# Splitting operands ahead of a stage boundary, and multiplying the first output tile there

## The chip, the cores and the metric

The kernel runs on one core of a Trainium2 chip. The metric is the device time of one execution in microseconds. Besides, one execution was recorded by the hardware profiler; its times are those of the profile.

## The reference

One step of a hybrid decoder layer on a prompt of 1024 tokens and on 8 samples of 4 tokens, all in float32. A combined input projection feeds a gated DeltaNet group (4 heads) and a differential attention group (4 heads). What the change touches is the step after it, in which the outputs of the eight heads are joined and multiplied with `w_out`:

```python
h = x + jnp.concatenate([o_g, o_d], axis=-1) @ w_out          # (L, 1024) @ (1024, 1024)
hn = _rmsnorm(h, ffn_norm_g)
u, new_ffn = _causal_dwconv(hn @ w_up, ffn_buf, ffn_conv_w, ffn_conv_b)
y = h + (jax.nn.silu(u[..., :D_FF]) * u[..., D_FF:]) @ w_down
```

## The kernel before

The kernel holds everything with features on the 128 partitions and tokens along the free axis: `T` = 1056 columns, of which the last 32 are the samples. It has four phases that follow each other with a barrier of all engines: projection, DeltaNet and attention of the prompt, `sample_stage`, and `output_and_mlp`. A product in float32 is made of three products of rounded parts: an operand is split into `hi` (a cast on ScalarE) and `lo` (a subtraction on VectorE), and TensorE adds hi·hi, hi·lo and lo·hi. `SEQ` is 1024, `TG` 352, `KT` 8, `H` 4.

`sample_stage` (L1750) computes the samples' DeltaNet and paged attention, and beside it normalises and gates the head outputs of the prompt in three groups of columns (`norm` on VectorE, `gate` on GpSimd). Each engine's order is written out by hand. Near its end TensorE does `multiply(0)`, `turn_map(1)`, `turn_out(0)`, `multiply(1, ...)`, `turn_out(1)`, `sum_few(1)`. Each of these waits in the queue for ScalarE or VectorE: `turn_out(1)` for `keep_out(1)` on ScalarE, and `sum_few(1)` for `add_rows(1)` on VectorE and `square_few(1)` on ScalarE. After it, `root_few(1)` and `norm_few(1)` end the phase. SyncE loads the first two tiles of `w_out` (`w_raw`, 512 KB each) during it. Before the barrier the stage splits weight tile 0 (L2362, L2575) and head 0 over all columns (L2366, L2579).

`output_and_mlp` (L2585) begins with the output projection, in 16 units. Unit u makes output tile u % 8 for the token half u // 8 (528 columns, `HB`), with 48 matmuls of 264 columns (L3452): 8 heads, three products, two PSUM banks. Weight tiles have two buffers: SyncE loads tile u once `low(u-2)` is done, ScalarE casts it (`high(u)`, L2936), VectorE subtracts (`low(u)`, L3152), and TensorE's `unit(u)` waits for `split_lo`. Here the heads 1 to 7 are split over all 1056 columns first (`o_high`, L2939, and `o_low`, L3178), while unit 0 follows head by head; then comes the split of tile 1. After a unit VectorE adds the residual (`residual(u)`) and sums squares (`gather(u)`). SyncE's queue at the phase's start, which the change leaves as it is:

```python
for u in range(NO):
    if u >= 2:
        load(u)
    if u < 2:
        for t in ((0,), range(1, KT))[u]:
            sp.dma_start(hT[:, t, :], x_scratch[:, t, :]).then_inc(x_in[u], 16)
    if u in ROWS_AT:
        load_rows(ROWS_AT.index(u))
```

So eight loads of x_scratch of 528 KB and three small loads of rows stand ahead of `load(2)`. At units 2, 4, 6 and 7 TensorE also transposes rows (`turn_rows`). The MLP's up-projection follows, then the down-projection.

Of the kernel before, what the change touches and what calls it, by code (L numbers as in the profile page):

```python
# [22 lines left out]
P = 128  # L23
D = 1024
KT = D // P
# [88 lines left out]
def hybrid_step(nc, i, o):  # L114
# [64 lines left out]
    held.append(S_out)  # L179
    phase(sample_stage, i, o, c, feat, ba, key_in, z_scratch, S_out, o_hi, o_lo)  # L180
    c["free"] = c["w_out_end"]
    phase(output_and_mlp, i, o, c, feat, o_hi, o_lo, o_at, feat_at, w_out_at, h_scratch, g_scratch, x_scratch)


# [1564 lines left out]

def sample_stage(nc, i, o, c, feat, ba, key_in, z_scratch, S_out, o_hi, o_lo, sem):  # L1750

# [22 lines left out]
        m.sb(f"s_{n}", [P, NS]) for n in ("ET", "A", "AT", "PT", "I_AT", "I_AA", "fold", "far"))  # L1774
    DT = m.sb("s_DT", [P, P])
    q_rows = m.sb("s_q_rows", [P, H, NB * WP])
    assert m.top >= c["free"] + 4 * T
# [33 lines left out]
    mask_few = mapT[0:NS, 0, 0:NBT * NR].rearrange("p (t r) -> p t r", t=NBT)  # L1811
    mask = m.sb("p_mask", [P, NBT, NS])
    sign_row = m.sb("p_sign_row", [1, P])
    sign = m.sb("p_sign", [P, 1])
# [4 lines left out]
    sq = [late.sb(f"o_sq{x}", [P, TG]) for x in range(2)] + [e[x][:, 0:TG] for x in range(2)]  # L1819
    sq_few = [sq[t][:, 0:H * SB * NL].rearrange("p (h n) -> p h n", h=H) for t in range(NBT)]  # L1820
    o_junk = sq[0][:, 0:DH]
# [4 lines left out]
    z_few = late.sb("o_z_few", [P, H, NS])  # L1826
    roots = late.sb("o_roots", [P, TG])
    roots_hi = [late.sb(f"o_roots_hi{x}", [P, TG], F32R) for x in range(2)]
    roots_lo = [late.sb(f"o_roots_lo{x}", [P, TG], F32R) for x in range(2)]
    head_out = [feat[:, t if t < H else 2 * H + t, :] for t in range(NH)]  # L1830
    zT = feat[:, 4 * H:5 * H, 0:SEQ]
    GROUPS = [slice(0, TG), slice(TG, 2 * TG), slice(2 * TG, SEQ), slice(SEQ, T)]

    bank_a, bank_b = m.ps("s_bank_a", [P, 512]), m.ps("s_bank_b", [P, 512])
    key_ps = [m.ps(f"p_key_ps{x}", [P, 512]) for x in range(2)]
# [20 lines left out]
    w_in, w_high = [sem(f"o_w_in{n}") for n in range(2)], sem("o_w_high")  # L1856
    gated_few, head_high = sem("o_gated_few"), sem("o_head_high")
    z_in, z_few_in, z_made, strip_zero, strip_made, spread_made = (
# [52 lines left out]
    with nc.Block() as block:  # L1911
# [115 lines left out]
        def _(pe):  # L2027
# [79 lines left out]
            def turn_delta():  # L2107
                pe.wait_ge(dve_done, DV["o_scaled"])
                nc.tensor.transpose(bank_b[:, 0:P], o_rows[:, :], c["ident"][:, :]).then_inc(pe_done, 1)

# [90 lines left out]
            def spread_roots(use):  # L2201
# [50 lines left out]
            turn_out(0)  # L2252
            multiply(1, (turn_delta, lambda: sum_few(0)))
            turn_out(1)
            sum_few(1)

        @block.scalar
        def _(act):
# [54 lines left out]
            for b in range(NB):  # L2313
# [36 lines left out]
            def square_few(t):  # L2350
                act.wait_ge(out_added, H * (t + 1))
                nc.scalar.activation(sq_few[t], few(t), ACT.Square).then_inc(few_squared, 1)

# [18 lines left out]
        def _(dve):  # L2372
# [74 lines left out]
            def delta_gate():  # L2447
                dve.wait_ge(pe_done, PE["o_turned"])
                dve.wait_ge(z_made, H + 1)
                nc.vector.scalar_tensor_tensor(out=feat[:, 0:H, SEQ:T], in0=bank_b[:, 0:P].rearrange("p (h t) -> p h t", h=H),  # L2450
                                               scalar=c["gain"][:, 0:1], in1=z_few[:, :, :], op0=ALU.mult, op1=ALU.mult
                                               ).then_inc(gated_few, 1)
# [79 lines left out]
            for b in range(NB):  # L2532
# [32 lines left out]
                if b == 5:  # L2565
                    add_state(6)
                    add_state(7)
                    keep_map(0)
            maxes(1)
# [12 lines left out]
    m.free()  # L2582


def output_and_mlp(nc, i, o, c, feat, o_hi, o_lo, o_at, feat_at, w_at, h_scratch, g_scratch, x_scratch, sem):  # L2585

# [44 lines left out]

    pair = [m.ps(f"f_pair{b}", [P, 2, 512]) for b in range(4)]
    bank = [pair[b // 2][:, b % 2, :] for b in range(8)]
# [115 lines left out]
    with nc.Block() as block:  # L2749
# [178 lines left out]
        def _(act):  # L2928
            act.sem_inc(split_hi, CREDIT + 1)

# [7 lines left out]
            def o_high(t):  # L2938
                nc.scalar.copy(o_hi[:, t, :], head_out[t]).then_inc(o_hi_done, 1)  # L2939

# [13 lines left out]
            def x_high(name, j):  # L2954
                hi, lo = xop[name]
                if name in ("P1", "P2", "P3"):
                    n, x = (j if name == "P1" else HK + j), (1 if name == "P3" else 0)
                    act.wait_ge(scaled_h, KT * x + n + 1)
                    src = hT[:, n, halves[x]]
                    if name != "P3":  # L2960
                        act.wait_ge(o_lo_done, KT - 1)
                elif name == "P5":
                    act.wait_ge(t1_made, j + 1)
                    src = t1[:, j, :]
                elif name == "P4":
                    act.wait_ge(t4_made, j + 1)
                    src = hT[:, HK + j, one]
                else:
                    act.wait_ge(t2_made if name == "P6" else t3_made, j + 1)
                    src = hT[:, j, one if name == "P6" else two]  # L2970
                if name in ("P5", "P7", "P4", "P3"):
                    act.wait_ge(unit_done, NO)
                if name == "P6":
                    act.wait_ge(o_lo_done, KT - 1)
                nc.scalar.copy(hi[:, j, :], src).then_inc(x_hi_done[name], 1)

            def up_high(s):
# [5 lines left out]
                if s < WR:  # L2983
                    if s >= 3:
                        act.wait_ge(unit_done, NO)
                    else:
                        act.wait_ge(rows_turned, 4)
                else:
                    act.wait_ge(multiplied, s - WR + 1)
                nc.scalar.copy(wop[s % WR][0][:, :, :], W_OF[name]).then_inc(up_hi, 1)  # L2990

            for t in range(1, KT):
                o_high(t)
            high(1)
            nc.scalar.preload_act_table(ACT.Sqrt)
            for u in range(NO):
                square_of(u)
                if u + 2 < NO:
                    high(u + 2)
                if u == KT:  # L3000
                    roots(0)
# [143 lines left out]
        def _(dve):  # L3145
            sub, add, mult = ALU.subtract, ALU.add, ALU.mult
            dve.sem_inc(split_lo, CREDIT + 1)

# [27 lines left out]
            def o_low(t):  # L3176
                dve.wait_ge(o_hi_done, t)
                nc.vector.tensor_tensor(o_lo[:, t, :], head_out[t], r32(o_hi[:, t, :]), sub).then_inc(o_lo_done, 1)  # L3178

# [235 lines left out]
        def _(pe):  # L3415
# [25 lines left out]
            def unit(u):  # L3441
# [4 lines left out]
                for k in range(KT):  # L3446
                    if u == 0 and k:
                        pe.wait_ge(o_lo_done, k)
                    for x, (w, t) in enumerate(PARTS):
                        for b in range(2):  # L3450
                            a = half * HB + b * HQ
                            mm = nc.tensor.matmul(pair[s][:, b, 0:HQ], (w_hi, w_lo)[w][s][:, k, :], (o_hi, o_lo)[t][:, k, a:a + HQ],  # L3452
                                                  start=(k + x == 0), stop=(k == KT - 1 and x == 2))
# [169 lines left out]
```

## Time and profile before

| what | value |
|---|---|
| time, median of 3 runs | 1624.13 us (1623.47 to 1630.41) |
| the profiled execution | 1628.96 us |
| its span | 1627.4 us |
| TensorE matmuls busy | 1515.5 us, 93% |
| VectorE busy | 1054.6 us, 65% |
| ScalarE busy | 638.4 us, 39% |
| GpSimd busy | 395.5 us, 24% |
| mean granted TensorE clock | 0.968 |

The span runs from the first to the last recorded instruction; the rest of an execution lies around it. Times in the rows count from the start of the span. The granted clock is 1.00 at the full 2.4 GHz and 0.50 at 1.2 GHz.

### The profile page before, as it was taken

To read this page: it belongs to the slowest core of one execution; us is meant where nothing else is said; L and a number is where in the kernel's file an instruction comes from. 1 tells how busy PE (TensorE), PEld (TensorE's weight loads), DVE (VectorE), ACT (ScalarE), POOL (GpSimd) and SP (SyncE) were. 2 spreads that over 40 slices of the span, in tenths; PEclk is the share of its full clock that TensorE was granted. 3 is DMA by queue.
4 is the path that set the end of the run, shared out by engine and by line. 5 is a ranking of instruction groups with operands and counts; after the bars stand their busy time and mean duration, and the time that the engine had idled before them with its cause. 6 is when DMAs were issued, how large, how long until landed. Compare 5 with 4: busy or idle time off the path is not lost.

```text
span 1627.4 us, 30132 instructions
## 1 busy us (share of the span) xinstructions
PE 1515.5 (93%) x11911; PEld 1430.0 (88%) x11911; DVE 1054.6 (65%) x1575; ACT 638.4 (39%) x1102; POOL 395.5 (24%) x750
## 2 busy tenths in 40 slices
PE   7999999898688888788999799999999999999998
PEld 6999999898577777644898799999999999999998
DVE  7444389777557676456547988887878787534420
ACT  6434242332334443353423444444444445423222
POOL 4000166554432243153002322222222220000000
PEclk8999999999789999899899799999999999999999
DMA  6211111232112311185542122222222226745333
GB/s 220 97 48 52 28 47 35 87 100 92 31 37 54 105 25 38 46 328 156 193 148 93 53 78 79 71 78 72 77 80 79 82 92 207 262 159 198 132 107 108
DMA packets 177981, 165.63 MB, mean 102 GB/s; under 512 B 24245, under 2 KB 157163, under 8 KB 176184
## 3 DMA queue, kind: packets, MB, share of 16 engines
q1 hardware_dynamic: 173528, 154.30, 30.7%
q0 software_dynamic: 1664, 6.29, 1.0%
q10 hardware_dynamic: 2656, 3.21, 0.5%
q8 instruction: 90, 1.47, 0.4%
q14 instruction: 43, 0.35, 0.1%
HBM read 125.68 MB, written 37.96 MB: 101 GB/s over the span
## 4 chain that ended last, share of the span: by engine, by line
PE 47%; DVE 2%; issue 1%; DMA 1%; ACT 1%; SPq 0%; POOL 0%; ACTq 0%; DVEq 0%; POOLq 0%
PE f_pair L3498 27%; PE f_pair L3544 15%; PE f_pair L3452 3%; DMA w_raw<-in_w_out 1%; DVE feat L3194 0%; PE f_pair L3578 0%; ACT w_hi L2936 0%; DVE m_xP_lo L3208 0%; DMA up_raw<-in_w_up 0%; DVE feat L3213 0%; SPq L2800 0%; PE f_pair L3512 0%; PE f_pair L3421 0%; DVE feat L3160 0%; DVE w_lo L3152 0%
## 5 line engine op out<-in xcount | busy, mean ns | idle before, releaser
L3498 PE MATMUL f_pair<-m_xP_hi,up_w_hi 128*128 128x264 f32 x1232 | 254.6, 288 | 12.8 <-DVE m_xP_lo L3208 9.4
L3498 PE MATMUL f_pair<-m_xP_lo,up_w_hi 128*128 128x264 f32 x1232 | 252.5, 286 | 0.0
L3498 PE MATMUL f_pair<-m_xP_hi,up_w_lo 128*128 128x264 f32 x1232 | 252.3, 286 | 0.0
L195 PE MATMUL proj<-x_hi,win_hi 128*128 128x352 f32 x672 | 220.1, 327 | 0.0
L195 PE MATMUL proj<-x_hi,win_lo 128*128 128x352 f32 x672 | 217.3, 323 | 0.0
L195 PE MATMUL proj<-x_lo,win_hi 128*128 128x352 f32 x672 | 216.9, 323 | 0.0
L3498 PEld LDWEIGHTS f_pair<-m_xP_hi,up_w_hi 128*128 128x128 f32 x1232 | 192.9, 190 | 15.3 <-issue 10.2
L3498 PEld LDWEIGHTS f_pair<-m_xP_lo,up_w_hi 128*128 128x128 f32 x1232 | 193.0, 190 | 0.0
L3498 PEld LDWEIGHTS f_pair<-m_xP_hi,up_w_lo 128*128 128x128 f32 x1232 | 192.5, 190 | 0.0
L3544 PE MATMUL f_pair<-dn_g_hi,dn_w_hi 128*128 128x352 f32 x528 | 171.9, 325 | 0.2 <-DVE f_pre L3271 0.2
L3544 PE MATMUL f_pair<-dn_g_lo,dn_w_hi 128*128 128x352 f32 x528 | 169.7, 321 | 0.0
L3544 PE MATMUL f_pair<-dn_g_hi,dn_w_lo 128*128 128x352 f32 x528 | 169.4, 321 | 0.0
L195 PEld LDWEIGHTS proj<-x_lo,win_hi 128*128 128x128 f32 x672 | 127.7, 190 | 0.0
L195 PEld LDWEIGHTS proj<-x_hi,win_hi 128*128 128x128 f32 x672 | 127.3, 189 | 0.3
L195 PEld LDWEIGHTS proj<-x_hi,win_lo 128*128 128x128 f32 x672 | 127.3, 189 | 0.0
L769 DVE RECIPROCAL head_root<-head_root 128x352 f32<-128x352 f32 x48 | 112.5, 2345 | 15.5 <-ACT head_root L591 15.3
L3319 DVE SCALAR_TENSOR_TENSOR f_acc<-f_pre,f_col,f_acc 128x1072 f32<-128x1072 f32 x88 | 116.8, 1329 | 0.0
L3355 DVE TENSOR_TENSOR dn_w_lo<-dn_raw,dn_w_hi 128x1024 fp32r<-128x1024 f32 x50 | 61.2, 1224 | 69.9 <-ACT dn_g_hi L3097 69.5
L3544 PEld LDWEIGHTS f_pair<-dn_g_lo,dn_w_hi 128*128 128x128 f32 x528 | 100.0, 189 | 0.0
L3544 PEld LDWEIGHTS f_pair<-dn_g_hi,dn_w_hi 128*128 128x128 f32 x528 | 99.0, 187 | 0.5 <-DVE f_pre L3271 0.5
L3231 DVE TENSOR_TENSOR up_w_lo<-up_sums,up_w_hi 128x512 fp32r<-128x512 f32 x88 | 72.0, 820 | 42.2 <-ACT up_w_hi L2990 42.2
L3544 PEld LDWEIGHTS f_pair<-dn_g_hi,dn_w_lo 128*128 128x128 f32 x528 | 99.1, 188 | 0.0
(462 smaller groups left out, 2932.3 us busy)
## 6 DMA issues: line engine op xcount, KB each, us to landing
dn_raw<-in_w_down SPq DMA_DIRECT2D x50, 512.0 KB, 4.0
up_raw<-in_w_up SPq DMA_DIRECT2D x44, 512.0 KB, 4.6
win_raw<-in_w_in SPq DMA_DIRECT2D x28, 512.0 KB, 3.9
g_scratch<-f_prod SPq DMA_DIRECT2D x22, 528.0 KB, 2.7
dn_g_in<-g_scratch SPq DMA_DIRECT2D x66, 176.0 KB, 3.6
p_key<-in_cache_k SPq DMA_DIRECT2D x32, 256.0 KB, 3.7
w_raw<-in_w_out SPq DMA_DIRECT2D x16, 512.0 KB, 6.1
x_scratch<-feat SPq DMA_DIRECT2D x1, 4224.0 KB, 12.0
```

The lines of the kernel that those rows point to most:

```text
L195: mm = nc.tensor.matmul(out, w[:, k, :], x[:, k, g * TG:(g + 1) * TG], start=(k == 0 and i == 0), stop=(k == KT - 1 and i == 2))
L769: nc.vector.reciprocal(root[j % 2][:, :], root[j % 2][:, :]).then_inc(root_inverted, 1)
L3231: nc.vector.tensor_tensor(lo[:, :, :], W_OF[order(s // NP)[s % NP]], r32(hi[:, :, :]), sub).then_inc(up_lo, 1)
L3319: nc.vector.scalar_tensor_tensor(out=acc[s][:, 0:F_OUT], in0=pre[s][:, t:t + F_OUT], scalar=col[:, j, NB * F_PAD + t:NB * F_PAD + t + 1], ...
L3355: nc.vector.tensor_tensor(dw[s][1][:, 0, :], w_in[NTH_W[u] % NRAW][:, :], r32(dw[s][0][:, 0, :]), sub)
L3452: mm = nc.tensor.matmul(pair[s][:, b, 0:HQ], (w_hi, w_lo)[w][s][:, k, :], (o_hi, o_lo)[t][:, k, a:a + HQ], start=(k + x == 0), stop=(k == ...
L3498: mm = nc.tensor.matmul(pair[OF[name]][:, b, 0:HQ], w_[a][:, j, :], x_[t][:, j, b * HQ:(b + 1) * HQ], start=(name in FIRST_IN and j + x == ...
L3544: mm = nc.tensor.matmul(bank[f][:, 0:TG], w_[a][:, 0, f * P:(f + 1) * P], g_[t][:, 0, :], start=(k == KS[g][0] and x == 0), stop=(k == KS[ ...
```

## The change

The phase `sample_stage` now splits the first 528 columns of all eight heads (`split_one` on ScalarE and VectorE) and both loaded weight tiles, and TensorE does all of unit 0 in it (`first_unit`), in three pieces around `turn_out(1)` and `sum_few(1)`. Its PSUM tile `pair0` outlives the barrier. The sample stage's transposed DeltaNet output moves to another bank for this. `output_and_mlp` starts with the residual of unit 0 and with unit 1, and splits the second 528 columns of the heads one by one behind units 0 to 7 (`two_hi`, `two_lo`), since only unit 8 needs them. On ScalarE `high(2)` comes first there.

```diff
+    c["pair0"] = shared.ps("f_pair0", [P, 2, 512])
...
+            def first_unit(a, b):
+                if a == 0:
+                    pe.wait_ge(w_low, 1)
+                    pe.wait_ge(dve_done, DV["S7"])
+                for k in range(a, b):
+                    pe.wait_ge(one_low, k + 1)
+                    for x, (w, o_) in enumerate((("w_hi", one_hi), ("w_hi", one_lo), ("w_lo", one_hi))):
+                        for y in range(2):
+                            nc.tensor.matmul(c["pair0"][:, y, 0:HQ], c[w][0][:, k, :], o_[k][:, y * HQ:(y + 1) * HQ],
+                                             start=(k + x == 0), stop=(k == KT - 1 and x == 2))
...
             multiply(1, (turn_delta, lambda: sum_few(0)))
+            first_unit(0, 2)
             turn_out(1)
+            first_unit(2, 4)
             sum_few(1)
+            first_unit(4, KT)
...
+            def split_one(t):
+                act.wait_ge(gated, (2 if t < H else NG) * H)
+                act.wait_ge(normed, NH * 2)
+                if t >= H:
+                    act.wait_ge(fresh_scored, 2)
+                nc.scalar.copy(one_hi[t][:, :], head_out[t][:, 0:HB]).then_inc(one_high, 1)
+
+            for t in range(H):
+                split_one(t)
             exps(1)
+            for t in range(H, NH):
+                split_one(t)
             keep_out(0)
...
             root_few(0)
             act.wait_ge(gated_few, 1)
-            act.wait_ge(gated, H * NG)
-            nc.scalar.copy(o_hi[:, 0, :], head_out[0]).then_inc(head_high, 1)
+            act.wait_ge(normed, NH * NG)
+            act.wait_ge(w_in[1], 16)
+            nc.scalar.copy(c["w_hi"][1][:, :, :], c["w_raw"][1][:, :, :]).then_inc(w_high, 1)
             keep_out(1)
...
+            split_one(0)
+            split_one(1)
             maxes(1)
+            split_one(2)
             weigh(1)
+            split_one(3)
+            split_one(4)
             keep_map(1)
             add_rows(0)
             delta_norm()
-            dve.wait_ge(w_high, 1)
-            nc.vector.tensor_tensor(c["w_lo"][0][:, :, :], c["w_raw"][0][:, :, :], r32(c["w_hi"][0][:, :, :]), ALU.subtract)
+            split_one(5)
+            split_w(0)
             delta_gate()
             norm_few(0)
-            dve.wait_ge(head_high, 1)
-            nc.vector.tensor_tensor(o_lo[:, 0, :], head_out[0], r32(o_hi[:, 0, :]), ALU.subtract)
+            split_one(6)
+            split_one(7)
             add_rows(1)
+            split_w(1)
             norm_few(1)
...
         @block.scalar
         def _(act):
-            act.sem_inc(split_hi, CREDIT + 1)
+            act.sem_inc(split_hi, CREDIT + 2)
...
-            for t in range(1, KT):
-                o_high(t)
-            high(1)
+            high(2)
             nc.scalar.preload_act_table(ACT.Sqrt)
             for u in range(NO):
                 square_of(u)
-                if u + 2 < NO:
+                if 1 <= u < NO - 2:
                     high(u + 2)
+                if u < KT:
+                    o_high(u)
...
-            for t in range(1, KT):
-                o_low(t)
-            low(1)
             for u in range(NO):
                 residual(u)
                 gather(u)
                 if u + 2 < NO:
                     low(u + 2)
+                if u < KT:
+                    o_low(u)
...
                 for k in range(KT):
-                    if u == 0 and k:
-                        pe.wait_ge(o_lo_done, k)
+                    if u == KT:
+                        pe.wait_ge(o_lo_done, k + 1)
...
+            pe.sem_inc(unit_done, 1)
             for u in range(NO):
-                unit(u)
+                if u:
+                    unit(u)
```

## Rows read from the trace of the kernel before

**Rows 1.** The page, busy time of each engine.

```profile
PE 1515.5 (93%) x11911; PEld 1430.0 (88%) x11911; DVE 1054.6 (65%) x1575; ACT 638.4 (39%) x1102; POOL 395.5 (24%) x750
```

**Rows 2.** The chain that ended last: start, duration, what.

```profile
774.32 0.33 SPq L2800
...
779.53 10.37 DMA w_raw<-in_w_out
...
789.93 1.06 ACT w_hi L2936
791.01 1.24 DVE w_lo L3152
...
792.29 6.19 PE f_pair L3452 x48
...
905.36 5.97 PE f_pair L3498 x24
...
912.18 3.16 PE f_pair L3498 x24
```

**Rows 3.** Windows: stretch, its length, busy time by engine, granted clock, DMA share, GB/s.

```profile
774.40:784.90 10.50, 9.70 (x48) 9.02 (x48) 9.40 (x9) 9.14 (x9) 0.00 (x0) 0.63 0.92 357
784.90:792.20 7.30, 6.15 (x48) 5.93 (x48) 1.86 (x4) 1.69 (x2) 0.00 (x0) 1.00 0.90 241
792.20:884.80 92.60, 92.06 (x768) 91.12 (x768) 52.91 (x73) 29.67 (x44) 2.59 (x2) 1.00 0.42 131
...
774.40:782.20 7.80, 7.08 (x30) 6.77 (x31) 6.70 (x6) 7.80 (x8) 0.00 (x0) 0.50 0.88 335
905.40:911.90 6.50, 5.94 (x24) 5.33 (x24) 5.79 (x8) 6.47 (x12) 0.99 (x1) 0.50 0.00 0
...
342.00:345.20 3.20, 3.20 (x13) 3.20 (x12) 3.17 (x3) 0.33 (x1) 2.24 (x4) 0.50 0.55 150
771.90:774.40 2.50, 0.00 (x0) 0.00 (x0) 0.84 (x2) 0.32 (x2) 0.00 (x0) 0.51 0.00 0
```

**Rows 4.** DMA issues, 784 to 786 us: count, KB each, us from issue to landing.

```profile
w_raw<-in_w_out SPq DMA_DIRECT2D x1, 512.0 KB, 6.8
```

**Rows 5.** Timeline, end of the sample stage: start, duration, engine, line; in brackets idle time before.

```profile
768.60 0.60 PE L2174 MATMUL p_score<-p_key,p_mapT 128*32 128x512 f32 x2
768.70 1.26 DVE L2579 TENSOR_TENSOR o_lo<-feat,o_hi 128x1056 fp32r<-128x1056 f32 x1
769.26 0.59 ACT L2286 COPY p_e<-p_score 128x512 f32<-128x512 f32 x1 [0.59 <-PE p_score L2174]
...
769.90 0.66 PE L2184 MATMUL p_fresh_ps<-ident,p_e 128*128 128x128 f32 x4 [0.71 <-ACT p_e L2286]
770.60 0.48 DVE L2502 TENSOR_REDUCE feat<-p_fresh_ps 128x16 f32<-128x32 f32 x4 [0.64 <-PE p_fresh_ps L2184]
...
771.42 0.43 PE L2113 MATMUL p_key_ps<-o_sq,ones 128*128 128x64 f32 x2 [0.87 <-ACT o_sq L2352]
...
772.83 0.28 DVE L2458 SCALAR_TENSOR_TENSOR feat<-feat,gain,o_roots_few 128x64 f32<-128x64 f32 x1
...
774.41 0.81 PE L3452 MATMUL f_pair<-o_hi,w_hi 128*128 128x264 f32 x2 [2.55 <-DVEq L3147]
```

**Rows 6.** Instructions of two lines: count, shortest/median/longest ns, first and last start.

```profile
L2975 ACT CAST m_xP_hi<-feat x24: 626/628/632, 853.6 to 913.5; 128x528 fp32r<-128x528 f32 x24
...
L3208 DVE TENSOR_TENSOR m_xP_lo<-feat,m_xP_hi x24: 694/701/1814, 856.3 to 918.5; 128x528 fp32r<-128x528 f32 x24
```

**Rows 7.** Timeline of ScalarE and VectorE, 755 to 763 us, idle times where splits go.

```profile
758.67 0.69 ACT L2279 ACTIVATE p_e<-p_score,p_stat 128x512 f32<-128x512 f32 x1 [4.47 <-DVE p_stat L2474]
...
762.15 0.59 ACT L2286 COPY p_e<-p_score 128x512 f32<-128x512 f32 x1 [2.40 <-PE p_score L2174]
...
757.56 0.19 DVE L2469 TENSOR_TENSOR p_fresh<-p_fresh_ps,p_mask 128x32 f32<-128x32 f32 x1 [1.43 <-PE p_fresh_ps L2156]
...
762.81 0.88 DVE L2491 COPY p_mapT<-p_score 128x128 f32<-128x128 f32 x4 [1.94 <-PE p_fresh_ps L2164]
```

More of the change, by code:

```diff
@@ L179, in hybrid_step @@
     held.append(S_out)
-    phase(sample_stage, i, o, c, feat, ba, key_in, z_scratch, S_out, o_hi, o_lo)
+    shared = Memory(nc, keep.top)
+    c["pair0"] = shared.ps("f_pair0", [P, 2, 512])
+    phase(sample_stage, i, o, c, feat, feat_at, ba, key_in, z_scratch, S_out)
     c["free"] = c["w_out_end"]
-    phase(output_and_mlp, i, o, c, feat, o_hi, o_lo, o_at, feat_at, w_out_at, h_scratch, g_scratch, x_scratch)
+    phase(output_and_mlp, i, o, c, feat, o_at, feat_at, w_out_at, h_scratch, g_scratch, x_scratch)
 def ln_rows(ap):
@@ L1747, in delta_and_attention, with sample_stage @@
     m.free()
-def sample_stage(nc, i, o, c, feat, ba, key_in, z_scratch, S_out, o_hi, o_lo, sem):
+def sample_stage(nc, i, o, c, feat, feat_at, ba, key_in, z_scratch, S_out, sem):
     o_part = 4 * KT * T
@@ L1775, in sample_stage @@
     DT = m.sb("s_DT", [P, P])
+    q_rows_at = m.top
     q_rows = m.sb("s_q_rows", [P, H, NB * WP])
@@ L1796, in sample_stage @@
     NV = NB - 2
+    keyT_at = m_low.top
     keyT = [over_split.sb("p_keyT0", [P, H, PAST]), m_low.sb("p_keyT1", [P, H, PAST])]
@@ L1812, in sample_stage @@
     mask = m.sb("p_mask", [P, NBT, NS])
+    sign_at = m.top
     sign_row = m.sb("p_sign_row", [1, P])
@@ L1819, in sample_stage @@
     sq = [late.sb(f"o_sq{x}", [P, TG]) for x in range(2)] + [e[x][:, 0:TG] for x in range(2)]
-    sq_few = [sq[t][:, 0:H * SB * NL].rearrange("p (h n) -> p h n", h=H) for t in range(NBT)]
+    sq_few = [m.at(f"o_sq_few{t}", [P, H, SB * NL], F32, sign_at + 4 * H * SB * NL * t)[:, :, :] for t in range(NBT)]
     o_junk = sq[0][:, 0:DH]
@@ L1827, in sample_stage @@
     roots = late.sb("o_roots", [P, TG])
+    roots_at = late.top
     roots_hi = [late.sb(f"o_roots_hi{x}", [P, TG], F32R) for x in range(2)]
@@ L1830, in sample_stage @@
     head_out = [feat[:, t if t < H else 2 * H + t, :] for t in range(NH)]
+    HB = T // 2
+    HQ = HB // 2
+    ONE_LO = [q_rows_at + 4 * HB * x for x in range(2)] + [roots_at + 4 * HB * x for x in range(3)] + [keyT_at + 4 * HB * x for x in range(3)]
+    one_hi = [m.at(f"o_one_hi{t}", [P, HB], F32R, feat_at + 4 * T * (4 * H + t % H) + 4 * HB * (t // H)) for t in range(NH)]
+    one_lo = [m.at(f"o_one_lo{t}", [P, HB], F32R, at) for t, at in enumerate(ONE_LO)]
+    c["o_one"] = (one_hi, one_lo)
     zT = feat[:, 4 * H:5 * H, 0:SEQ]
     GROUPS = [slice(0, TG), slice(TG, 2 * TG), slice(2 * TG, SEQ), slice(SEQ, T)]
-    bank_a, bank_b = m.ps("s_bank_a", [P, 512]), m.ps("s_bank_b", [P, 512])
+    bank_a, bank_b = c["pair0"][:, 0, :], c["pair0"][:, 1, :]
     key_ps = [m.ps(f"p_key_ps{x}", [P, 512]) for x in range(2)]
@@ L1856, in sample_stage @@
     w_in, w_high = [sem(f"o_w_in{n}") for n in range(2)], sem("o_w_high")
-    gated_few, head_high = sem("o_gated_few"), sem("o_head_high")
+    gated_few, w_low = sem("o_gated_few"), sem("o_w_low")
+    one_high, one_low = sem("o_one_high"), sem("o_one_low")
     z_in, z_few_in, z_made, strip_zero, strip_made, spread_made = (
@@ L2108, in turn_delta @@
                 pe.wait_ge(dve_done, DV["o_scaled"])
-                nc.tensor.transpose(bank_b[:, 0:P], o_rows[:, :], c["ident"][:, :]).then_inc(pe_done, 1)
+                nc.tensor.transpose(key_ps[1][:, P:2 * P], o_rows[:, :], c["ident"][:, :]).then_inc(pe_done, 1)
             def sum_few(t):
@@ L2351, in square_few @@
                 act.wait_ge(out_added, H * (t + 1))
+                act.wait_ge(setup_ps, 1)
                 nc.scalar.activation(sq_few[t], few(t), ACT.Square).then_inc(few_squared, 1)
@@ L2449, in delta_gate @@
                 dve.wait_ge(z_made, H + 1)
-                nc.vector.scalar_tensor_tensor(out=feat[:, 0:H, SEQ:T], in0=bank_b[:, 0:P].rearrange("p (h t) -> p h t", h=H),
+                nc.vector.scalar_tensor_tensor(out=feat[:, 0:H, SEQ:T], in0=key_ps[1][:, P:2 * P].rearrange("p (h t) -> p h t", h=H),
                                                scalar=c["gain"][:, 0:1], in1=z_few[:, :, :], op0=ALU.mult, op1=ALU.mult
@@ L2568, in _, with split_one, split_w @@
                     keep_map(0)
+            def split_one(t):
+                dve.wait_ge(one_high, t + 1)
+                if t < 2:
+                    dve.wait_ge(pe_done, PE["qS"])
+                elif t < 5:
+                    dve.wait_ge(normed, NH * NG)
+                else:
+                    dve.wait_ge(scored, NB)
+                nc.vector.tensor_tensor(one_lo[t][:, :], head_out[t][:, 0:HB], r32(one_hi[t][:, :]), ALU.subtract).then_inc(one_low, 1)
+            def split_w(n):
+                dve.wait_ge(w_high, n + 1)
+                if n:
+                    dve.wait_ge(gated_few, 1)
+                    dve.wait_ge(normed, NH * NG)
+                nc.vector.tensor_tensor(c["w_lo"][n][:, :, :], c["w_raw"][n][:, :, :], r32(c["w_hi"][n][:, :, :]), ALU.subtract).then_inc(w_low, 1)
+            split_one(0)
+            split_one(1)
             maxes(1)
+            split_one(2)
             weigh(1)
+            split_one(3)
+            split_one(4)
             keep_map(1)
@@ L2573, in _, with output_and_mlp @@
             delta_norm()
-            dve.wait_ge(w_high, 1)
-            nc.vector.tensor_tensor(c["w_lo"][0][:, :, :], c["w_raw"][0][:, :, :], r32(c["w_hi"][0][:, :, :]), ALU.subtract)
+            split_one(5)
+            split_w(0)
             delta_gate()
             norm_few(0)
-            dve.wait_ge(head_high, 1)
-            nc.vector.tensor_tensor(o_lo[:, 0, :], head_out[0], r32(o_hi[:, 0, :]), ALU.subtract)
+            split_one(6)
+            split_one(7)
             add_rows(1)
+            split_w(1)
             norm_few(1)
     m.free()
-def output_and_mlp(nc, i, o, c, feat, o_hi, o_lo, o_at, feat_at, w_at, h_scratch, g_scratch, x_scratch, sem):
+def output_and_mlp(nc, i, o, c, feat, o_at, feat_at, w_at, h_scratch, g_scratch, x_scratch, sem):
     m = Memory(nc, c["free"])
@@ L2630, in output_and_mlp @@
     tail_tok = m.at("f_tail_tok", [F_TAIL, 2, 4 * P], F32, h_at + 7 * 4 * T - 4320 - 4096)
-    pair = [m.ps(f"f_pair{b}", [P, 2, 512]) for b in range(4)]
+    pair = [c["pair0"]] + [m.ps(f"f_pair{b}", [P, 2, 512]) for b in range(1, 4)]
+    o_two = [m.at(f"o_two_{x}", [P, KT, HB], F32R, o_at + at) for x, at in (("hi", 7840), ("lo", 40160))]
+    two_hi, two_lo = o_two
     bank = [pair[b // 2][:, b % 2, :] for b in range(8)]
@@ L2938, in o_high @@
             def o_high(t):
-                nc.scalar.copy(o_hi[:, t, :], head_out[t]).then_inc(o_hi_done, 1)
+                nc.scalar.copy(two_hi[:, t, :], head_out[t][:, two]).then_inc(o_hi_done, 1)
             def square_of(u):
@@ L2960, in x_high @@
                     if name != "P3":
-                        act.wait_ge(o_lo_done, KT - 1)
+                        act.wait_ge(o_lo_done, KT)
+                        act.wait_ge(unit_done, KT)
                 elif name == "P5":
@@ L2973, in x_high @@
                 if name == "P6":
-                    act.wait_ge(o_lo_done, KT - 1)
+                    act.wait_ge(o_lo_done, KT)
                 nc.scalar.copy(hi[:, j, :], src).then_inc(x_hi_done[name], 1)
@@ L2986, in up_high @@
                     else:
+                        act.wait_ge(unit_done, KT)
                         act.wait_ge(rows_turned, 4)
@@ L3146, in _ @@
             sub, add, mult = ALU.subtract, ALU.add, ALU.mult
-            dve.sem_inc(split_lo, CREDIT + 1)
+            dve.sem_inc(split_lo, CREDIT + 2)
             def low(u):
@@ L3176, in o_low @@
             def o_low(t):
-                dve.wait_ge(o_hi_done, t)
-                nc.vector.tensor_tensor(o_lo[:, t, :], head_out[t], r32(o_hi[:, t, :]), sub).then_inc(o_lo_done, 1)
+                dve.wait_ge(o_hi_done, t + 1)
+                nc.vector.tensor_tensor(two_lo[:, t, :], head_out[t][:, two], r32(two_hi[:, t, :]), sub).then_inc(o_lo_done, 1)
             def inverse(x):
@@ L3446, in unit @@
                 for k in range(KT):
-                    if u == 0 and k:
-                        pe.wait_ge(o_lo_done, k)
+                    if u == KT:
+                        pe.wait_ge(o_lo_done, k + 1)
                     for x, (w, t) in enumerate(PARTS):
+                        o_ = o_two[t][:, k, :] if half else c["o_one"][t][k][:, :]
                         for b in range(2):
-                            a = half * HB + b * HQ
-                            mm = nc.tensor.matmul(pair[s][:, b, 0:HQ], (w_hi, w_lo)[w][s][:, k, :], (o_hi, o_lo)[t][:, k, a:a + HQ],
+                            mm = nc.tensor.matmul(pair[s][:, b, 0:HQ], (w_hi, w_lo)[w][s][:, k, :], o_[:, b * HQ:(b + 1) * HQ],
                                                   start=(k + x == 0), stop=(k == KT - 1 and x == 2))
                 mm.then_inc(unit_done, 1)
+            pe.sem_inc(unit_done, 1)
             for u in range(NO):
-                unit(u)
+                if u:
+                    unit(u)
                 if u in ROWS_TURN:
```

## The prediction

> **What bounds the kernel now.** The page comes first: TensorE is busy 93% of the span [rows 1], so it looks as if 6 us of matmuls moved to an earlier place must be worth something near 6 us. The average says nothing about the place, so the next view is the chain of waits, between 774 and 800 us, where the output stage begins. It does not run through TensorE there. It runs from SyncE's first issue at 774.32, through the load of w_raw for unit 2, issued at 779.53 and landed 10.37 us later, then ScalarE's cast (1.06) and VectorE's subtraction (1.24), and only at 792.29 into the matmuls of unit 2 [rows 2]. So from the first issue to unit 2 are 17.97 us that hold no matmul. The windows show the rest: units 0 and 1 lie between 774.4 and 792.2 and keep TensorE busy for 9.70 and 6.15 us. From 792.2 to 884.8 it is busy 92.06 of 92.6 us [rows 3]. There any delay of TensorE goes to the end one for one, and any time saved ahead of it counts only if unit 2 starts earlier.
>
> Why is the load so late? SyncE issues it behind eight loads of x_scratch (4.3 MB) and three of f_rows, and the DMA engines are 92% busy at 357 GB/s in that stretch [rows 3]. The change touches no line of this queue ahead of load(2). In the row for the next one, load(3), issue to landing is 6.8 us [rows 4].
>
> **The end of the sample stage.** The timeline by engine shows its last steps. The last matmuls of multiply(1) start at 768.60 and end at 769.20. ScalarE then copies the rows (769.26), TensorE transposes them (769.90), VectorE adds (770.60), TensorE sums squares (771.42), and VectorE's last multiplication ends at 772.83 + 0.28 = 773.11. TensorE starts the next stage at 774.41 [rows 5]. TensorE's free time in this tail is what the change wants to fill: 773.11 − 769.20 = 3.9 us less 0.66 + 0.43 for its own steps, 2.8 us.
>
> **The change, part by part.**
>
> Splits added to the sample stage: eight casts of 528 columns on ScalarE at 0.63 us and eight subtractions on VectorE at 0.70 us [rows 6]. Four casts go in front of exps(1), where ScalarE sits idle 4.47 us; 4 x 0.63 = 2.5 us fits. Four go behind it, into 2.40 us before keep_out(0) at 762.15, which with 2.5 us is up to 0.1 us late [rows 7]. The copy it makes is needed by turn_out(0), behind which TensorE has no work until map_kept at VectorE's end; I count nothing. If that cover were gone, it would cost 0.1 us. VectorE's pair ahead of maxes(1) (1.4 us) meets 1.43 us of idle time, the one ahead of weigh(1) the wait for the exps, the next two (1.4 us) the 1.94 us before keep_map(1) [rows 7]. The last two take the place of the old subtraction of 1.26 us at 768.70 [rows 5]: 0.14 us more, before add_rows(1), which waits for TensorE anyway. Sum: 0, at worst 0.3.
>
> Second weight tile: cast and subtraction (1.06 + 1.24 us [rows 2]) move ahead of the stage boundary. The cast takes the slot of the old o_hi cast. The subtraction stands between add_rows(1) and norm_few(1), where VectorE waits for the sum of squares and its root. 0, at worst 0.2.
>
> The 48 matmuls of first_unit: the unit measured between 784.9 and 792.2 takes 6.15 us at full clock [rows 3], 0.128 each. They stand in TensorE's queue as 12, turn_out(1), 12, sum_few(1), 24. In order from 769.20: 12 of them to 770.74, so turn_out(1) starts 0.84 us later than its 769.90; behind it wait add_rows(1), the squares and the sum. 12 more from 771.40 to 772.94, so sum_few(1) is at 772.94 instead of 771.42, and VectorE's last step ends at 774.6. The last 24 run from 773.37 to 776.44, after everything else. The stage ends 776.44 − 773.11 = 3.3 us later. The ends of matmuls in these rows overlap the next one's start by some 0.1 to 0.2 us at each of the steps, so I take +3.0; bounds 2.5 and 3.7 (the latter with the 0.3 and a part of the 0.2 above). Equally: 6.15 us of work less 2.8 us of room is 3.3.
>
> Removed from the output stage: unit 0 (9.70 us at mostly half clock), seven full casts and seven subtractions of o_hi and o_lo, and the split of tile 1. None of them ends last before unit 2, since the chain shows only SyncE, the DMA and the split of tile 2. **Worth 0.** The chain of 17.97 us starts with the boundary and moves with it. load(3) no longer waits for low(1) and is issued some 5 us sooner, but behind load(2), in the same queue. If it took bandwidth from load(2) for the whole overlap, 512 KB at 357 GB/s are 1.5 us; I take 0.
> The Trainium skill says in "DMA: Bandwidth & Descriptors", section "Queues, rings and completion order", that descriptors of one queue are consumed in ring order on each engine, though completions can pass each other. By it the term is 0 too, and the sum stays.
>
> Second halves of the heads: eight casts and subtractions go between units 0 to 7. Per unit VectorE would have two additions and one subtraction over 528 columns, at the 0.70 of [rows 6], and 1.24 for a tile, 3.3 us in a unit of 6.2. The tightest is unit 3: cast 3 now follows load 2's split, the table load and two squares, and ends about 2 us later than before, still before unit 2 ends at +6.2. 0.
>
> What is late next: TensorE. With unit 1 ready at once, it runs from the new start for 6.15 us, and then has nothing for 17.9 − 6.2 = 11.7 us. Before, it waited 1.2 us there. In this trace such pauses cost clock: with no matmul from 771.9 to 774.4 the granted clock is at its lower level, 1.2 GHz, and stays there for 7.8 us of the new work. After the thin stretch before 905.4 it is low for 6.5 us more [rows 3]. In the chain the first 24 matmuls after that pause take 5.97 us and 24 later ones 3.16 [rows 2]: 2.8 us lost. Unit 2 stands at the head of the 92 us that are full, so this loss goes to the end. I take 2.8, the row it is nearest to. Bounds: 0 if the clock did not fall, 1.6 by the stretch 342.0 to 345.2 (3.2 us at half), 3.9 by 7.8 us at half.
> The Trainium skill, "TensorE: Matmul & The Clock Gate", section "HAM oscillation — how this bites in real kernels", tells that a wait for a DMA sets the clock back and the next group starts cold. It speaks against this change; were it wrong here, the sum would be +3.0 instead of +5.8, and the rows above side with it.
>
> **Sum.** +3.0 (boundary) + 0 (removed work) + 2.8 (clock) = +5.8 us. The profiled execution took 1628.96 us (span 1627.4 and 1.56 around it), so its like would take 1634.8. The median of the runs is 1624.13, 4.83 below; on it the sum gives 1629.9, 0.36% more.
>
> **Rivals.**
> *No loss of clock* (0.17): the clock stays up or comes back at once. For: the pause of 7.30 − 6.15 = 1.15 us before unit 2 leaves it at 1.00 [rows 3]. Against: 11.7 us without a matmul is more than any stretch here that kept it. +3.0, 1627.1.
> *Unit 2 does not wait for the load* (0.05): if the load landed before unit 1 ends, the stage would give back 792.29 − (777.4 + 6.15) = 8.7 us of its 17.97 and cost nothing in clock, 1615.4. It decides from a landing 2.3 us before 783.6, some 9 us sooner than 789.9 + 3.0. Against: 4.3 MB stand ahead of it.
> *Nothing is left of it* (0.05): the matmuls fit into the tail with the boundary unmoved and the clock kept; 1624 to 1625. Against: 2.8 us of room for 6.15.
> *The clock falls inside the tail* (0.12), the slower side: before, it fell at 771.9. Should it do so with the new matmuls there, the last 24 take 6.2 us instead of 3.1, and the sum is 3.0 + 3.1 + 2.8 = 8.9, 1633.0 (+0.55%). It decides if the clock is low for more than 4.6 us of the tail. Against: TensorE now has work from 769.2 on without a pause.
> The forecast has 0.58, things not named 0.03.
>
> **How the numbers follow.** 1629.9 is the likeliest case. Its own range by its bounds (2.5 + 1.6 to 3.7 + 3.9) is 1628.2 to 1631.7. The range given adds the case without loss of clock below and the fall in the tail above, and something for the scatter of the runs, which spans 7 us: 1625.3 to 1634.2. Some 0.5% (8 us) is what a measurement of this kernel can tell from no change. Faster by more than that is the second rival, 0.05; slower by more is the fourth and a part of the forecast's upper edge, 0.15; within it 0.80.
>
> **What the changed profile would show.** Right: the last matmul of the sample stage at about 776.2 and the first issue of SyncE 3 us later than 774.3; issue to landing of load(2) at 10 us again; about 18 us from that first issue to unit 2; 11 to 12 us of idle TensorE before unit 2, ended by w_lo; unit 2's first matmuls at about twice the 0.128 us each. Wrong: unit 2 less than 17 us after the first issue, or a granted clock of 1.00 through unit 2, or casts or subtractions that hold up exps(1), keep_map(1) or turn_out(1) by more than 0.3 us. A chain that leads into unit 3 through w_lo would show a split that I put at nothing.

## The result, and the profile after

The changed kernel takes 1633.33 us in the median of 20 runs, the kernel before 1626.57 us in 20 runs. The ratio is 1.0034, 95% interval 1.0021 to 1.0047. That is 5.5 us more (0.0034 x 1626.57; the two medians as they stand are 6.8 us apart), where +5.8 us was forecast. It is clear of no change, and inside the 0.5% that was called no difference. The profiled execution of the changed kernel took 1631.33 us, its span is 1629.7 us. Its first stages happened to be 2 to 3 us shorter than in the profile of before (the sample stage's first memset is at 681.6 us, before at 684.4), so what follows compares distances, not positions.

The chain of waits of the changed kernel, from SyncE's first issue of the output stage (start, duration, what):

```profile
774.89 0.33 SPq L2865
...
779.98 11.59 DMA w_raw<-in_w_out
791.57 0.02 issue
791.59 1.05 ACT w_hi L3001
792.65 0.02 issue
792.67 1.24 DVE w_lo L3219
793.90 0.04 issue
793.95 7.55 PE f_pair L3518 x48
801.50 0.79 PE f_pair L3487 x11
802.29 11.86 PE f_pair L3518 x96
```

It is the chain of before [rows 2]: SyncE, the load of tile 2, its split, unit 2. Unit 0 is gone from the stage, and unit 2 still starts 793.95 − 774.89 = 19.06 us after the first issue, before 17.97. The windows say what TensorE does there (stretch, length, busy time of PE, PEld, DVE, ACT, POOL, granted clock, DMA share, GB/s):

```profile
775.00:781.30 6.30, 6.06 (x48) 5.89 (x48) 0.71 (x1) 0.00 (x0) 0.00 (x0) 1.00 0.86 314
781.30:793.90 12.60, 0.00 (x0) 0.00 (x0) 1.23 (x1) 2.29 (x2) 0.00 (x0) 0.59 0.85 280
793.90:801.50 7.60, 7.55 (x49) 7.41 (x50) 3.88 (x5) 3.32 (x6) 0.00 (x0) 0.79 0.23 69
801.50:887.00 85.50, 85.48 (x720) 84.73 (x720) 53.73 (x74) 30.80 (x46) 2.57 (x2) 1.00 0.44 136
```

Unit 1 runs alone at full clock. Then TensorE waits 12.8 us for w_lo, and in this wait the granted clock falls. Unit 2 starts at 1.2 GHz, as its two parts show:

```profile
793.90:797.10 3.20, 3.15 (x14) 3.15 (x15) 1.33 (x2) 1.80 (x5) 0.00 (x0) 0.50 0.51 153
797.20:801.50 4.30, 4.30 (x36) 4.15 (x36) 2.53 (x3) 1.42 (x2) 0.00 (x0) 1.00 0.02 6
```

It takes 7.55 us instead of 6.19. From there on TensorE is full again, as in [rows 3], and the loss goes to the end.

The tail of the sample stage on TensorE's timeline (start, duration, engine, line; in brackets the idle time before):

```profile
766.39 0.60 PE L2187 MATMUL p_score<-p_key,p_mapT 128*32 128x512 f32 x2
766.91 0.51 PE L2234 MATMUL f_pair<-o_one_hi,w_hi 128*128 128x264 f32 x2
...
768.49 0.60 PE L2197 MATMUL p_fresh_ps<-ident,p_e 128*128 128x128 f32 x4
...
770.39 0.33 PE L2126 MATMUL p_key_ps<-o_sq_few,ones 128*128 128x64 f32 x2
...
773.29 0.41 PE L2234 MATMUL f_pair<-o_one_hi,w_lo 128*128 128x264 f32 x2
775.08 0.48 PE L3518 MATMUL f_pair<-o_one_hi,w_hi 128*128 128x264 f32 x2 [1.38 <-DVEq L3214]
```

From the start of multiply(1)'s last matmuls, turn_out(1) comes after 768.49 − 766.39 = 2.10 us (before 1.30 [rows 5]), sum_few(1) after 4.00 (before 2.82), and the last 24 matmuls end at 773.70. SyncE's first issue follows after 774.89 − 766.39 = 8.50 us, before 774.32 − 768.60 = 5.72. **The boundary is 2.8 us later.** VectorE's last multiplication ends sooner than TensorE, at 771.69 + 0.28 = 771.97, so the last 24 matmuls end the stage, as the prediction had it:

```profile
771.69 0.28 DVE L2498 SCALAR_TENSOR_TENSOR feat<-feat,gain,o_roots_few 128x64 f32<-128x64 f32 x1
```

That the splits cost nothing ahead of it shows on ScalarE's timeline:

```profile
756.45 0.69 ACT L2306 ACTIVATE p_e<-p_score,p_stat 128x512 f32<-128x512 f32 x1 [2.34 <-DVE p_stat L2514]
...
759.94 0.58 ACT L2313 COPY p_e<-p_score 128x512 f32<-128x512 f32 x1 [0.28 <-PE p_score L2187]
```

and on VectorE's:

```profile
755.35 0.19 DVE L2509 TENSOR_TENSOR p_fresh<-p_fresh_ps,p_mask 128x32 f32<-128x32 f32 x1 [0.19 <-PE p_fresh_ps L2169]
...
760.60 0.88 DVE L2531 COPY p_mapT<-p_score 128x128 f32<-128x128 f32 x4 [0.71 <-PE p_fresh_ps L2177]
```

The idle times of [rows 7] (4.47, 2.40, 1.43 and 1.94 us) have shrunk to 2.34, 0.28, 0.19 and 0.71, and each step is still released by what released it before. From VectorE's step at 755.35 to the start of multiply(1)'s last matmuls it is 766.39 − 755.35 = 11.04 us, before 768.60 − 757.56 = 11.04.

### The profile page after: what moved, and what is told of

Read it like the earlier page. It is cut to its first block, busy times and chain, and to the rows that moved or that the text cites. A ratio compares the mean times of both kernels' runs of the same rounds, so it can differ in the third digit from the quotient of the medians.

```text
span 1629.7 us, 30169 instructions
## 1 busy us (share of the span) xinstructions
PE 1508.9 (93%) x11911; PEld 1425.8 (87%) x11911; DVE 1053.7 (65%) x1583; ACT 639.0 (39%) x1110; POOL 394.6 (24%) x750
## 4 chain that ended last, share of the span: by engine, by line
PE 48%; DVE 1%; issue 1%; DMA 1%; ACT 0%; SPq 0%; POOL 0%; ACTq 0%; DVEq 0%; POOLq 0%
PE f_pair L3566 27%; PE f_pair L3612 15%; PE f_pair L3518 5%; DMA w_raw<-in_w_out 1%; PE f_pair L3646 0%; DVE feat L3280 0%; SPq L2865 0%; PE f_pair L3580 0%; PE f_pair L3487 0%; DVE feat L3261 0%; DVE m_xP_lo L3275 0%; DVE dn_w_lo L3421 0%; ACT y_rows L3209 0%; DVE feat L3282 0%; DVE f_pre L3337 0%
```

## Experiments

Distances in the profiles of all kernels, in us. A: from multiply(1)'s last matmuls to SyncE's first issue of the output stage. B: from the issue of load(2) to its landing. C: TensorE idle before unit 2. D: the matmuls of unit 2. E: from multiply(1)'s last matmuls to the last instruction of the span, so everything behind the place of the change. A dash marks a load that was not read because nothing on the path waited for it. E comes from one profile of each kernel, but it leaves out what varies ahead of the change: the changed kernel and hold_load3, which differ in nothing that is waited for, have 863.3 and 863.2. The runs of the experiments were taken in three groups, beside runs of the kernel before with medians of 1626.13, 1627.62 and 1627.43 us, so the ratios can be compared with each other, and the medians only roughly.

| kernel | A | B | C | D | E | median us | ratio to before |
|---|---|---|---|---|---|---|---|
| before | 5.7 | 10.37 | 1.2 | 6.19 | 858.8 | 1626.57 | |
| changed | 8.5 | 11.59 | 12.8 | 7.55 | 863.3 | 1633.33 | 1.0034 [1.0021, 1.0047] |
| hold_load3 | 8.5 | 11.48 | 12.6 | 7.58 | 863.2 | 1631.38 | 1.0034 [1.0020, 1.0048] |
| unit0_back | 5.7 | 10.63 | 3.6 | 7.62 | 859.9 | 1628.27 | 1.0012 [1.0000, 1.0025] |
| filled_wait | 8.5 | 11.54 | 1.9 | 6.11 | 861.4 | 1632.07 | 1.0040 [1.0025, 1.0056] |
| loads_first | 8.5 | 6.18 | 3.15 | 8.71 | 854.3 | 1620.28 | 0.9961 [0.9948, 0.9975] |
| x_early | 8.5 | 4.43 | 1.6 | 6.09 | 850.3 | 1618.09 | 0.9938 [0.9925, 0.9952] |
| before_x_early | 5.7 | – | 0 | 12.09 for units 1 and 2 | 856.6 | 1626.42 | 0.9992 [0.9981, 1.0003] |
| unit1_held | 8.5 | 10.50 | 0 | 13.39 for units 1 and 2 | 866.2 | 1632.52, one run | |
| x_early_w_first | 8.5 | 4.33 | 0.55 | 6.11 | 849.6 | 1619.28 | 0.9942 [0.9927, 0.9956] |
| x_early_unit0_back | 5.7 | – | 0 | 19.76 for units 0 to 2 | 853.5 | 1624.01 | 0.9975 [0.9964, 0.9986] |

**hold_load3.** Does the earlier load(3) make load(2) late?

```diff
                     sp.wait_ge(split_lo, done(u - 2))
+                if u == 3:
+                    sp.wait_ge(loaded[0], 16)
```

> The changed kernel, with load(3) issued only when load(2) has landed. Theory A (the earlier load(3) takes DMA bandwidth from load(2)): load(2) lands 10.4 us after its issue as before, instead of 11.59, and unit 2 starts some 1.2 us sooner after the stage's first issue; in time 1.2 us under the changed kernel's 1633.3, about 1632. Theory B (the 11.59 us are scatter, loads are served in order): landing and time as in the changed kernel.

Load(2) landed after 11.48 us although load(3) was not yet issued. My theory A fell. The time did not move. Something else adds 1.1 us to the load; see unit1_held.

**unit0_back.** The splits stay in the sample stage, and the 48 matmuls go back.

```diff
-            first_unit(0, 2)
             turn_out(1)
-            first_unit(2, 4)
             sum_few(1)
-            first_unit(4, KT)
...
-            pe.sem_inc(unit_done, 1)
             for u in range(NO):
-                if u:
-                    unit(u)
+                unit(u)
```

> The changed kernel with the splits in the sample stage kept, but unit 0 multiplied in the output stage again. Theory A (the 48 matmuls push the boundary, and the wait for load(2) gives nothing back): the stage boundary is some 3 us sooner after multiply(1) than in the changed kernel, unit 2 starts at the same distance from the boundary, TensorE waits 5 to 6 us there instead of 12.8, and the time falls by 3 us or more, to 1629 or 1630; a loss of clock at unit 2 may stay. Rival (the splits themselves or the new order on ScalarE and VectorE cost the time): the time stays near 1633.

The boundary is back at 5.7 us, the landing at 10.63, and the ratio falls from 1.0034 to 1.0012, 3.6 us. So the move of the 48 matmuls is the larger part of what the change costs. The 5 to 6 us of waiting that I expected were 3.6: units 0 and 1 take 14.36 us there, at a mean granted clock of 0.81. Unit 2 still pays for the clock (7.62 us, 1.4 more than before). So the splits hold nothing up, but by making units 0 and 1 ready early they lengthen the wait for load(2), and this, with 0.3 us of the landing, is about what is left (0.0012, 2.0 us, with an interval that reaches to nothing).

**filled_wait.** 88 matmuls whose result nobody reads keep TensorE at work while load(2) is awaited (NFILL is 88).

```diff
+                if u == 1:
+                    for n in range(NFILL):
+                        nc.tensor.matmul(bank[7][:, 0:HQ], c["o_one"][0][0][:, 0:P], c["o_one"][0][1][:, 0:HQ], start=True, stop=True)
```

> The changed kernel with 88 extra matmuls (264 columns, result not used) behind unit 1, which keep TensorE at work while load(2) is awaited. Theory A (the pause costs clock): the granted clock stays at 1.00 through unit 2, whose 48 matmuls take 6.1 us instead of 7.55; the time falls by 1.4 to 2.8 us, to about 1631. Rival (the pause costs nothing beyond itself): unit 2 and the time are unchanged within 1 us.

The windows, of which the second holds the added work (columns as above):

```profile
775.00:781.00 6.00, 6.00 (x51) 6.00 (x51) 0.71 (x1) 0.00 (x0) 0.00 (x0) 1.00 0.93 339
781.00:793.40 12.40, 10.56 (x86) 10.35 (x84) 1.19 (x1) 2.25 (x2) 0.00 (x0) 1.00 0.87 280
793.40:799.60 6.20, 6.11 (x49) 5.98 (x50) 3.91 (x6) 3.36 (x6) 0.00 (x0) 1.00 0.30 87
```

The clock stays at 1.00 and unit 2 takes 6.11 us. The pause therefore costs 7.55 − 6.11 = 1.4 us in the profile. E is 1.9 us less than in the changed kernel. The timed runs don't show the fall that I expected: the ratio is 1.0040, and its interval overlaps most of that of the changed kernel, so 1.4 us can be neither shown nor excluded by them.

**loads_first.** SyncE's order is turned round, so that tile 2 no longer stands behind the whole of x_scratch. The residual of unit 0 waits for two tiles of it, that of unit 2 for the rest.

```diff
-                if u >= 2:
+                if u >= 4:
                     load(u)
-                if u < 2:
-                    for t in ((0,), range(1, KT))[u]:
-                        sp.dma_start(hT[:, t, :], x_scratch[:, t, :]).then_inc(x_in[u], 16)
+                if u == 0:
+                    for t in range(2):
+                        sp.dma_start(hT[:, t, :], x_scratch[:, t, :]).then_inc(x_in[0], 16)
+                    load(2)
+                    load(3)
                 if u in ROWS_AT:
                     load_rows(ROWS_AT.index(u))
+                if u == 1:
+                    for t in range(2, KT):
+                        sp.dma_start(hT[:, t, :], x_scratch[:, t, :]).then_inc(x_in[1], 16)
...
-                if u < 2:
-                    dve.wait_ge(x_in[u], 16 * (KT - 1) if u else 16)
+                if u == 0:
+                    dve.wait_ge(x_in[0], 32)
+                if u == 2:
+                    dve.wait_ge(x_in[1], 16 * (KT - 2))
```

> The changed kernel with SyncE's order turned round: two tiles of x_scratch, then load(2) and load(3), the rows, and then the six other tiles of x_scratch; the residual of unit 2 waits for these. Theory A (the place of load(2) in the queue sets unit 2): load(2) lands some 5 us after its issue, unit 2 starts 8 to 10 us after the stage's first issue instead of 19.06, the clock stays up, and the time falls by 9 to 12 us, to about 1622, under the kernel before (1626.6). Rival (something else holds unit 2 or the next units, such as the x tiles being late for the residual of unit 2): the gain is under 5 us and the chain runs through the residual.

Its chain of waits:

```profile
770.00 6.18 DMA w_raw<-in_w_out
...
776.20 1.05 ACT w_hi L3006
...
777.27 1.24 DVE w_lo L3224
...
778.55 8.71 PE f_pair L3525 x48
```

Unit 2 starts 778.55 − 769.14 = 9.4 us after the first issue, and the kernel is faster than the one before. I had the clock wrong: it fell in a pause of only 3.15 us, and unit 2 took 8.71 us, 2.6 more than at full clock (columns as above):

```profile
775.60:778.50 2.90, 0.00 (x0) 0.00 (x0) 1.22 (x1) 2.28 (x2) 0.00 (x0) 0.84 1.13 276
777.60:784.40 6.80, 5.85 (x26) 5.85 (x27) 4.61 (x6) 4.22 (x6) 0.00 (x0) 0.50 1.00 387
```

**x_early.** The eight loads of x_scratch move into the sample stage, behind multiply(0), whose values lay in their place. Their semaphores outlive the boundary.

```diff
+    held.extend(c["x_in"])
...
+            sp.wait_ge(multiplied, 1)
+            for t in range(KT):
+                sp.dma_start(feat[:, H + t, :], c["x_scratch"][:, t, :]).then_inc(c["x_in"][t > 0], 16)
             sp.wait_ge(state_out, 16)
...
-                if u < 2:
-                    for t in ((0,), range(1, KT))[u]:
-                        sp.dma_start(hT[:, t, :], x_scratch[:, t, :]).then_inc(x_in[u], 16)
```

> The changed kernel with the eight loads of x_scratch issued in the sample stage, once multiply(0) has read the values that lay in their place. Theory A: load(2) is then alone with load(3) and the rows, lands about 5 us after the stage's first issue, unit 2 follows unit 1 within 1 or 2 us at full clock, and the time falls by 12 to 14 us against the changed kernel, to about 1620. Rival: the loads, now beside the store of the state, hold up the end of the sample stage or are still under way behind the boundary, and less than half of it is gained.

Its chain of waits:

```profile
778.95 4.43 DMA w_raw<-in_w_out
...
783.40 1.06 ACT w_hi L3004
...
784.49 1.24 DVE w_lo L3222
...
785.77 6.09 PE f_pair L3521 x48
791.86 0.79 PE f_pair L3490 x11
```

Unit 2 starts 7.9 us after the first issue at 777.90, 1.6 us behind unit 1, with the clock at 1.00:

```profile
785.70:791.90 6.20, 6.13 (x50) 6.00 (x50) 3.90 (x7) 3.34 (x6) 0.00 (x0) 1.00 0.29 85
```

The ratio falls from 1.0034 to 0.9938, which is 15.6 us, above the 12 to 14 that I expected; E falls by 13.0. The boundary did not get later (A is 8.5).

**before_x_early.** The same early loads in the kernel before.

> The kernel before with the same early loads of x_scratch and nothing else changed. Theory A: units 0 and 1 (9.7 and 6.15 us of matmuls) are now what unit 2 waits for, so only the 1.2 us of its wait for the load can be gained, 1625 or 1626. Then the change under study is worth 5 to 6 us once the loads are out of the way. Rival (the early loads alone are worth most of it, whatever is split or multiplied before the boundary): 1621 or less.

1.3 us (0.08%), as theory A said; the interval reaches to no change. Its chain of waits runs through the splits of the heads now:

```profile
773.02 6.83 DVE o_lo L3181 x6
779.85 0.19 issue
780.04 1.25 DVE o_lo L3181
781.29 1.15 DVE w_lo L3155
...
782.48 12.09 PE f_pair L3455 x96
```

So either measure alone gives nothing, the early loads 0.0008 and the change −0.0034, and both give 0.0062. With the loads out of the way the change is worth 0.9992 − 0.9938 = 0.0054, 8.8 us by the timed runs. From the two intervals I estimate 6 to 11.6 us for this difference, and the profiles side with the lower end: E is 856.6 − 850.3 = 6.3 us less, 6.0 of it by the end of unit 2. So the 5 to 6 us that I expected were not far off, and what the other 2.5 us are stays open.

**unit1_held.** What makes load(2) late? One row of the DMA view differs. The view lists packets by queue (packets, MB, share of 16 engines); first the changed kernel, from SyncE's first issue to 786.5:

```profile
q1 hardware_dynamic: 1088, 4.13, 92.3%
q8 instruction: 1, 0.02, 0.5%
```

and then the kernel before, 774.3 to 786.5:

```profile
q1 hardware_dynamic: 1199, 4.41, 92.8%
```

One packet of the instruction queue (16 KB, 1.0 us on one of the 16 DMA engines, at 783.38 in the changed kernel) falls among the x_scratch loads in the changed kernel, hold_load3 and filled_wait. In the kernel before (791.08) and in unit0_back it comes behind the landing. To move it, TensorE was kept from beginning unit 1 before load(2) has landed:

```diff
+                if u == 1:
+                    pe.wait_ge(loaded[0], 16)
                 if u:
                     unit(u)
```

> The changed kernel in which TensorE does not begin unit 1 before load(2) has landed. In five profiles load(2) landed 11.48 to 11.59 us after its issue where one 16 KB packet of the instruction queue came 7 to 9 us after SyncE's first issue, between the x_scratch packets, and 10.37 or 10.63 us where that packet came behind the landing. Theory C (the packet belongs to TensorE's code, which the changed kernel reaches sooner, and it holds up one DMA engine and with it load(2)): with unit 1 held the packet comes behind the landing, and load(2) lands after 10.4 to 10.7 us. Rival (the 1.1 us come from something else in the changed kernel, the packet is chance): it lands after 11.5 us. The time itself must get longer, since unit 1 now stands behind the landing.

Its chain of waits:

```profile
778.46 10.50 DMA w_raw<-in_w_out
...
789.00 13.39 PE f_pair L3518 x96
```

The packet came at 795.47 and load(2) landed after 10.50 us. The windows from the first issue to the landing, first of the changed kernel and then of this one (columns as above), show that VectorE and ScalarE do the same work in both; of the engines that calculate only TensorE differs:

```profile
774.90:791.60 16.70, 6.06 (x48) 5.89 (x48) 0.71 (x1) 0.01 (x1) 0.00 (x0) 0.76 0.96 328
773.20:789.00 15.80, 0.00 (x0) 0.00 (x0) 0.71 (x1) 0.02 (x1) 0.00 (x0) 0.56 0.98 333
```

So theory C held, with one profile of each kernel: when TensorE gets ahead of its old place in the code, a packet of instructions comes while the loads run, and load(2) lands some 1 us later. That the packet carries TensorE's code follows from its moving with TensorE; that the one DMA engine which carries it is late with its share of the load is my reading, since the trace doesn't name the engine. As expected the kernel itself did not gain: E is 2.9 us longer than in the changed kernel, and the one timed run, 1632.52, tells nothing.

**x_early_w_first** issues load(2) and load(3) ahead of the rows.

> The changed kernel with the early loads of x_scratch, and load(2) and load(3) issued ahead of the three loads of rows. Theory: load(2) is issued 1.05 us sooner, unit 2 starts 1 us sooner behind unit 1, and the time falls by 1 us at most against x_early (1618.1), which the runs hardly tell. Rival (the rows, which are transposed behind unit 2, now come late): unit 2 starts sooner but the row transposes behind it wait, and nothing is gained.

C fell from 1.6 to 0.55 us, and E by 0.7. The ratio, 0.9942 against 0.9938, tells nothing from x_early, which remains the fastest median.

**x_early_unit0_back** is x_early with first_unit taken back as in unit0_back.

> The changed kernel with the early loads of x_scratch, and unit 0 multiplied in the output stage again. Theory: the boundary is 2.8 us sooner, but unit 0 (6.1 us, more at the lower clock behind the boundary) now stands on the path before unit 2, which is no longer set by the load; so the time is 3 to 6 us longer than x_early's 1618.1, 1621 to 1624. Rival (all of the gain of x_early over before_x_early comes from the splits in the sample stage, not from the matmuls moved): 1618 or less.

Its chain of waits behind the boundary:

```profile
778.45 19.76 PE f_pair L3518 x144
798.21 0.79 PE f_pair L3487 x11
```

The median is 5.9 us above x_early's, at the upper end. Units 0 to 2 stand in one row behind the boundary, and 19.76 us for 144 matmuls are 1.5 more than three times 6.09. The splits alone give 0.9992 − 0.9975 = 0.0017 (2.8 us) with early loads, the matmuls in the tail the other 0.0037 (6.0 us). The profiles agree on the splits (E 3.1 us less than in before_x_early) and not on the matmuls: there E differs by 853.5 − 850.3 = 3.2 us. The steps of the two chains give as much: against x_early, unit 0's 6.09 us and the 1.5 us come onto the path, the boundary's 2.8 and the pause of 1.6 leave it, 3.2 in sum. From the two intervals I estimate 3.2 to 8.8 us for the timed 6.0, so the timed runs do not contradict the profiles, but only 3.2 us are accounted for.

## Why the prediction was right, point by point

*The load sets unit 2, and removed work is worth 0.* Right. TensorE waited 12.8 us there for w_lo, and loads_first and x_early, which touch only the loads, brought 12 and 15.6 us. This is also where the expected gain went: it was off the path until the loads moved.

*The boundary, +3.0.* It measured 2.8, the same in every kernel with first_unit, and unit0_back took it away.

*The splits in the sample stage, 0.* Shown by the idle times left and by the 11.04 us that did not change. The whole stage tells less: from its first memset to multiply(1)'s last matmuls it is 84.2 us before and 84.8 in the changed kernel, but in the others it is 84.1 to 85.6 whether the splits are there or not, and 89.6 in unit1_held, whose sample stage is the changed kernel's.

*The landing of load(2), taken at 0.* Mis-sized: +1.2. I had named load(3) as what could cost up to 1.5 us, and hold_load3 showed that it costs nothing. By unit1_held the cost came with a packet of TensorE's own code, which the prediction did not know.

*The clock, 2.8 from a bound of 0 to 3.9.* The mechanism is shown by filled_wait, the size was twice too large: 7.55 − 6.19 = 1.4 us in the profile of the changed kernel. That is below 1.6, the least that the forecast's own range allowed for. In loads_first it was 2.6. In the changed kernel the clock was back after 3.2 us of unit 2, in loads_first only after 5.9, so the cost depends on when the clock falls and comes back, and one row of before was no good measure of it.

*The sum.* 2.8 + 1.2 + 1.4 = 5.4, against 3.0 + 0 + 2.8 = 5.8. So the total was right partly by luck: two errors of 1.2 and 1.4 us cancel. Read directly, unit 2 ends 801.50 − 766.39 = 35.1 us after multiply(1)'s last matmuls start, before 792.29 + 6.19 − 768.60 = 29.9, which is 5.2 us more, and E grows by 863.3 − 858.8 = 4.5. A small gain was not forecast: units 3 to 6 take 11.86 us in pairs instead of 12.01. Why their matmuls are a little shorter stays open.

*A wording.* The prediction says of the 17.97 us that they hold no matmul. That is true of the chain of waits alone: TensorE multiplies units 0 and 1 beside it. The sum did not use it.

*Rivals.* "No loss of clock" and "nothing is left of it" are excluded by the windows. "The clock falls inside the tail": it was at 1.00 throughout (58 matmuls, 6.8 us busy of 6.8 between 766.9 and 773.7). "Unit 2 does not wait for the load" was wrong here; x_early made it nearly true.

## What to carry to other kernels

Before work is moved ahead of a stage, look at which wait ends last before the stage's steady part, and follow it to the queue it comes from. Here the change cost 5.5 us while eight loads stood ahead of the one that counted, and gave 8.8 us (6.3 by the profiles) once they were gone. Moving work into another engine's waits costs what does not fit: 6.0 us into 3 us of room pushed the boundary by the rest. Two changes that are each worth nothing can be worth a lot together, so a null result deserves a look at what bounds the place now before it is dropped.

## What was unexpected in the hardware

TensorE's instruction stream shares the DMA engines with the data. Where one 16 KB packet of it, 1.0 us long, fell among the loads ahead, load(2) landed about 1 us later (11.48 to 11.59 us in three profiles, 10.37 to 10.63 in three where the packet came behind the landing), and the packet comes sooner when TensorE gets ahead. And the clock fell in a pause of 3.15 us: unit 2 of loads_first took 8.71 us, while after the pauses of 1.6 us in x_early and 1.9 us in filled_wait it took 6.09 and 6.11.
